# The first stage in feature tiles: rows scaled before they are turned, conditioning columns tile by tile, the first two wide tiles side by side

## The chip, the cores and the metric

The kernel runs on one core of a Trainium2 chip. Inside the core four compute engines work from queues of their own: PE (TensorE, matrix products, with its weight loads shown apart as PEld), DVE (VectorE), ACT (ScalarE) and POOL (GpSimd). SP (SyncE) issues nearly all transfers between HBM and the on-chip memory. The engines meet only at semaphores. The metric is the device time of one launch in microseconds (us); less is better.

## What is computed

One step of a decoder layer for 1024 prompt tokens and 8 sequences of 4 sample tokens, 1056 columns in all, in 32-bit floats. The change touches only what stands before the first wide product and the history that the convolution needs; shortened, the reference reads:

```python
mod = silu(c) @ w_ada + b_ada                    # c: 9 conditioning rows; w_ada: 1024 x 6144
sh1, sc1, g1, sh2, sc2, g2 = split(mod, 6)
h = rmsnorm(x, norm_mix_w) * (1 + sc1) + sh1
z = h @ w_in + b_in                              # 1024 x 8192: q, f, i, og, glu_a, glu_b, gate_a, gate_b
o_a, state = hgrn2_branch(q, f, i, og, lb, hgrn_norm_w, s0)          # 8 heads
o_b, buf = conformer_conv_branch(glu_a, glu_b, buf, dw_w, dw_b, ...) # depthwise, 31 taps, 30 rows of history
x = x + g1 * (concat(sigmoid(gate_a) * o_a, sigmoid(gate_b) * o_b) @ w_out)
h2 = rmsnorm(x, norm_ffn_w) * (1 + sc2) + sh2
gg, uu = split(h2 @ w_ffn_in, 2)
x = x + g2 * ((silu(gg) * uu) @ w_ffn_out)
y = rmsnorm(x, norm_final_w)
```

## The kernel before

Everything is kept feature-major: 128 features on the partitions, 1056 tokens along the free axis, and 8 such feature tiles (`j`) for the 1024 features. Every wide product is made in three passes of rounded operands, high times high, high times low and low times high, so h is needed as `h_hi` and `h_lo`, and each weight block of 1024 x 128 is loaded to `w_raw` (two buffers), rounded on ACT to `w_hi` (`hi`), and its rest is made as `w_lo` (`low`, on DVE in the loop, on POOL for block 0). One wide tile `z_tile` is one block: 8 rows `kt` of 9 products of 352 columns each (3 column groups, 3 passes), in one of the two PSUM tensors `Z`. A head has seven wide tiles, in the order glu_b, glu_a, i, q, f, og, gate_a, and there are 8 heads; tiles and blocks are numbered from 0 through the heads.

**The first stage.** SP loads the conditioning vectors, 9 row tiles `xrow` of x (four buffers), the small vectors, and the first 2048 columns of `w_ada` (`sh1` and `sc1`) in 8 pieces of 256 columns with two buffers `ada_w`. For each row tile PE turns the raw rows (transposes into `Z`, copied by DVE to `xt`), and then multiplies one `ada_w` piece: `ct`, the 9 columns of silu(c), is the stationary operand (a weight load of 9 columns) and 256 columns of `w_ada` stream past it. ACT squares the rows for the mean. Only after all of this come the turning of the conditioning rows, the roots, the row factors made into `ysum`, and then, feature tile by feature tile, h: DVE multiplies (`modulate`), ACT shifts and rounds (`shift_and_round`), POOL makes `h_lo`. The first wide tile waits row by row for `h_ready`; it is followed by the second.

**The order around it.** `load_block(b)` on SP waits for the split of the block whose buffer it takes; for block 1 the code waits for the split of block 0. After the loads SP copies the old history DRAM to DRAM, stores the turned history `ht` to `hist_dram` and x to `xt_dram`, waits for `h_ready` of all tiles, and then enters the loop of the heads (`body`), where behind block 2's place it loads `us`, the history of the head, and `aw`, a piece of `w_ada`. In the loop DVE walks through 28 slots per head, 4 per wide tile. After slot 8 (`CONV_SLOT`) every slot does two of the 31 taps of the convolution (`conv_tap`), until they are done. The recurrence of head h-1 runs in the slots of head h; its parts are small PE jobs between the rows of the wide tiles (`rec_fill`), which DVE and ACT empty. The DVE queue is strictly in the order of the code, so a `low` of the next block stands behind the taps of the tile before.

## Time and profile before

| | |
|---|---|
| Median of three runs | 2049.01 us (2047.14 to 2051.76) |
| Profiled execution, its own time | 2049.11 us |
| Its span in the profile | 2047.4 us |
| PE busy | 1968.2 us, 96% of the span |
| DVE, ACT, POOL busy | 1313.2, 666.9 and 245.4 us |
| Mean granted TensorE clock | 0.985 of full speed |
| First product of wide tile 0 / first product of wide tile 2 | 76.1 us / about 116 us |

The difference between span and time is 1.7 us. The span says how long the engines were at work from the first instruction to the last; the busy share of an engine is its mean over stages that have different limits, so a stage is read by itself: who is idle in it, and what ended each wait. A row of the timeline gives start, duration, engine, line, operation, what was written and read, and in square brackets how long the engine was idle before it and what released it.

### The profile page before, as it was taken

The numbers are of one execution on the slowest core, as the hardware profiler recorded it, in microseconds if no ns is written. First come the engines' busy times: TensorE is split into PE (matmuls) and PEld (weight loads), VectorE is DVE, ScalarE is ACT, GpSimd is POOL, SyncE is SP. The second block draws the span as 40 slices with busy tenths as digits, with TensorE's granted clock in tenths as the row PEclk, the third lists the DMA queues.
The fourth block names the chain that finished last, engine by engine and source line by source line (L and its number), as shares of the span: only waits on it lengthen the run. The fifth ranks groups of instructions, "written<-read, shape, count | busy, mean of one in ns | idle before, by whom it ended". The sixth has DMA issues, their size and how long they took to land.

```text
span 2047.4 us, 39363 instructions
## 1 busy us (share of the span) xinstructions
PE 1968.2 (96%) x15960; PEld 1886.6 (92%) x15960; DVE 1313.2 (64%) x1792; ACT 666.9 (33%) x1070; POOL 245.4 (12%) x245
## 2 busy tenths in 40 slices
PE   7699999999999999999989999999999999999997
PEld 3499999999999999998988989999999999999997
DVE  2776978787887878787575655545445554455444
ACT  2421222323131313132563333333333333333332
POOL 0430010101010001011131654700000000000000
PEclk9799999999999999999989999999999999999998
DMA  8422222223232232223267544444444544445442
GB/s 260 154 75 56 75 76 75 77 70 83 63 87 65 68 84 66 75 73 91 87 199 225 156 121 137 134 136 138 135 135 144 152 131 139 134 141 152 140 135 92
DMA packets 408485, 237.32 MB, mean 116 GB/s; under 512 B 16167, under 2 KB 402887, under 8 KB 408320
## 3 DMA queue, kind: packets, MB, share of 16 engines
q1 hardware_dynamic: 408336, 235.20, 38.9%
...
## 4 chain that ended last, share of the span: by engine, by line
PE 83%; DVE 8%; DMA 3%; ACT 3%; POOL 2%; issue 1%; SPq 0%; DVEq 0%; ACTq 0%; POOLq 0%
PE Z L809 72%; PE R L834 2%; PE R L756 1%; PE R L890 1%; DVE w_lo L1184 1%; DMA ada_w<-in_w_ada_dram 1%; ACT w_hi L1665 1%; PE R L840 1%; DMA w_raw<-in_w_out_dram 1%; DVE ta L1349 1%; PE R L916 1%; PE R L923 1%; DVE k L1213 1%; PE R L925 1%; DVE x L1553 1%
## 5 line engine op out<-in xcount | busy, mean ns | idle before, releaser
L809 PE MATMUL Z<-h_hi,w_hi 128*128 128x352 f32 x2592 | 695.5, 333 | 19.6 <-POOL h_lo L1954 17.0
L809 PE MATMUL Z<-h_hi,w_lo 128*128 128x352 f32 x2592 | 672.0, 323 | 0.0
L809 PE MATMUL Z<-h_lo,w_hi 128*128 128x352 f32 x2592 | 671.1, 323 | 0.0
L1665 ACT ACTIVATE w_hi<-w_raw 128x1024 fp32r<-128x1024 f32 (+1 forms) x316 | 329.4, 1043 | 944.3 <-PE Z L809 923.1
L1184 DVE TENSOR_TENSOR w_lo<-w_raw,w_hi 128x1024 fp32r<-128x1024 f32 (+1 forms) x306 | 376.5, 1230 | 383.8 <-ACT w_hi L1665 375.6
L809 PEld LDWEIGHTS Z<-h_hi,w_hi 128*128 128x128 f32 x2592 | 451.4, 189 | 39.6 <-issue 26.3
L809 PEld LDWEIGHTS Z<-h_hi,w_lo 128*128 128x128 f32 x2592 | 462.9, 189 | 0.0
L809 PEld LDWEIGHTS Z<-h_lo,w_hi 128*128 128x128 f32 x2592 | 461.1, 189 | 0.0
L1332 DVE SCALAR_TENSOR_TENSOR yb<-up,vec,yb 128x1024 f32 (+1 forms) x240 | 308.3, 1285 | 29.8 <-DVE yb L1332 3.7
L809 PE MATMUL Z<-act_hi,w_hi 128*128 128x352 f32 x528 | 170.4, 323 | 0.0
L809 PE MATMUL Z<-act_hi,w_lo 128*128 128x352 f32 x528 | 169.7, 321 | 0.0
L809 PE MATMUL Z<-act_lo,w_hi 128*128 128x352 f32 x528 | 169.5, 321 | 0.0
L809 PEld LDWEIGHTS Z<-act_hi,w_lo 128*128 128x128 f32 x528 | 99.4, 188 | 0.0
L2017 POOL TENSOR_TENSOR gate<-ta,tb 128x1056 f32<-128x1056 f32 x8 | 20.9, 2610 | 654.8 <-ACT ta L1727 654.8
L809 PEld LDWEIGHTS Z<-act_lo,w_hi 128*128 128x128 f32 x528 | 99.3, 188 | 0.0
L809 PEld LDWEIGHTS Z<-act_hi,w_hi 128*128 128x128 f32 x528 | 99.2, 188 | 0.0
L1586 DVE TENSOR_TENSOR tb<-ta,Z 128x352 f32<-128x352 f32 x66 | 34.4, 521 | 74.4 <-PE Z L809 74.2
L809 PE MATMUL Z<-m_hi_b,w_hi 128*128 128x352 f32 x192 | 64.9, 338 | 11.4 <-DVE w_lo L1184 8.8
L809 PE MATMUL Z<-m_hi_a,w_hi 128*128 128x352 f32 x192 | 63.8, 332 | 6.3 <-DVE w_lo L1184 4.0
L809 PE MATMUL Z<-m_hi_b,w_lo 128*128 128x352 f32 x192 | 63.9, 333 | 0.0
L809 PE MATMUL Z<-m_lo_b,w_hi 128*128 128x352 f32 x192 | 63.5, 331 | 0.0
L809 PE MATMUL Z<-m_hi_a,w_lo 128*128 128x352 f32 x192 | 63.2, 329 | 0.0
...
## 6 DMA issues: line engine op xcount, KB each, us to landing
w_raw<-in_w_ffn_in_dram SPq DMA_DIRECT2D x132, 512.0 KB, 3.8
w_raw<-in_w_in_dram SPq DMA_DIRECT2D x64, 512.0 KB, 5.0
w_raw<-in_w_out_dram SPq DMA_DIRECT2D x48, 512.0 KB, 4.0
w_raw<-in_w_ffn_out_dram SPq DMA_DIRECT2D x48, 512.0 KB, 3.8
aw<-in_w_ada_dram SPq DMA_DIRECT2D x32, 512.0 KB, 4.0
...
```

What stands on the lines that cost most here:

```text
L756: last = mm(R[n % 2][0:NSEQ, 0:2 * P], ct[:, kt, 0:NSEQ], ada_w[n % 2][:, kt, :], start=kt == 0, stop=kt == NJ - 1)
L809: last = mm(out, w[:, kt, :], x(kt, g), start=first and kt == 0 and m == 0, stop=last_block and kt == n - 1 and m == 2)
L834: return transpose(out, in_, ident[0:m, 0:m])
L840: last = mm(bank[group:group + 32, ADA_COL:ADA_COL + P], ct[:, kt, :], aw[:, kt, :], start=kt < 4, stop=kt >= 4)
L890: last = mm(bank[p:p + BAND, c * w:(c + 1) * w], k[:, t:t + BAND], halves(qd[:, t:t + BAND], 1 << lv, 1), start=True, stop=True)
L916: last = mm(bank[:, c * P:(c + 1) * P], ktok[:, cc, :], vtok[:, cc, :], start=True, stop=True)
L923: last = mm(out, att[:, cc, :], vtok[:, cc, :], start=True, stop=cc == 0)
L1184: st.tell(V.tensor_tensor(w_lo[b.par][:, 0:n, :], w_raw[b.par][:, 0:n, :], w_hi[b.par][:, 0:n, :].bitcast(F32), ALU.subtract), w_split, b. ...
L1332: ins = V.scalar_tensor_tensor(yp, xp, w, yp, ALU.mult, ALU.add)
L1586: st.tell(V.tensor_tensor(a, sg, Z[t.par][:, 1, 0:GW], ALU.mult), *zfree(t))
L1665: A(w_hi[b.par][:, 0:n, :], w_raw[b.par][:, 0:n, :], ACT.Copy).then_inc(w_hi_ready, 1)
L2017: st.tell(Q.tensor_tensor(gate[:, :], ta[:, :], tb[:, :], ALU.mult), gate_ready, h.v)
```

## The change

- **Rows are scaled token-major.** ACT squares a row tile; POOL makes the reciprocal root of its mean with a power (two instructions of one column per row tile); DVE scales the rows (`xn`, 128 x 1024). PE turns both the raw rows and the scaled rows; ACT copies the raw ones to `xt`, DVE the scaled ones to `xh`. The turning of the factors, the roots on ACT and `ysum` as a row of factors are gone.
- **Conditioning by feature tile.** `ada_w` holds, for one feature tile, 128 columns of `sh1` and 128 of `sc1`, in three buffers. PE multiplies with `w_ada` as the stationary operand (weight loads of 128 columns) and 9 columns of `ct` streaming: 16 products per feature tile. The result stands feature-major at once, so the 16 transposes of the conditioning rows are gone.
- **h by feature tile.** DVE adds the bias (two instructions), makes `am`, and forms h in a buffer from `xh`; ACT makes `h_hi` straight from `xh`; DVE, not POOL, makes `h_lo`. ACT rounds blocks 0 and 1 right after the first `h_hi`; POOL makes `w_lo` of both.
- **The first two wide tiles side by side.** After the conditioning of tiles 0 and 1, each step `kt` is: conditioning of tile `kt + 2`, row `kt` of wide tile 0, row `kt` of wide tile 1.
- **The history is moved.** Its turning stands in slots 8 to 11 of head 0 (the rows of wide tile 2), and in head 0 SP stores it and loads `us` after block 3 is issued, not before block 2. In head 0 DVE's sample part of the convolution stands in slot 14 and the taps begin in slot 12.
- SP issues the stores of x and the copy of the old history behind the last `ada_w` and `hrow` loads.

The diff, cut to its core:

```diff
-CONV_SLOT = 8
+CONV_SLOT, CONV_SLOT0, TAP_SLOT0 = 8, 14, 12
+N_TURNS = 2 * (NC + 1)
+XN = 8
+WADA = 3
+HIST_SLOT = 2 * SLOTS
...
+            def load_mod(j):
+                if j >= WADA:
+                    sp.wait_ge(ada_done, j - WADA + 1)
+                for sec in (SH1, SC1):
+                    sp.dma_start(ada_w[j % WADA][:, sec, :, :], wada_v[:, :, sec * D + j * P:sec * D + (j + 1) * P]) \
+                        .then_inc(adaw_loaded[j % WADA], 16)
...
+            load_mod(0)
+            for t in range(XBUF, NC + 1):
+                load_x(t)
+            load_mod(1)
+            for b in range(2):
+                load_block(Idx(b), win_v[:, :, ORDER[b] * D:ORDER[b] * D + P])
+            for j in range(2, NJ):
+                load_mod(j)
             old = state_conv[0].rearrange("(two s) w d -> two (s w) d", two=2)
             for m in range(2):
                 sp.dma_start(hrow[:, m, :], old[m]).then_inc(hrow_loaded, 16)
...
+            sp.wait_ge(x_evac, N_TURNS)
+            sp.dma_start(xt_dram.rearrange("j p t -> p j t"), xt[:, :, :]).then_inc(xt_stored, 16)
             sp.dma_start(cv_sample[0, :, 0:HIST - LS, :], state_conv[0, :, LS:HIST, :]).then_inc(hist_copied, 16)
...
+            sp.wait_ge(ada_done, NJ)
             sp.wait_ge(h_ready, NJ)
...
-                    if j == 1:
+                    if j == (3 if first else 1):
+                        if first:
+                            sp.wait_ge(hist_evac, 4)
+                            sp.dma_start(hist_dram.rearrange("j p w -> p j w"), ht[:, :, :]).then_inc(ht_stored, 16)
+                            sp.wait_ge(ht_stored, 16)
                         wait(sp, conv_done, h.v)
...
+            def conditioning(j):
+                pe.wait_ge(adaw_loaded[j % WADA], 32 * (j // WADA + 1))
+                if j < 2:
+                    pe.wait_ge(p0_evac, 2)
+                wait(pe, mod_read, j - 1)
+                for sec in (SH1, SC1):
+                    for kt in range(NJ):
+                        last = mm(R[j % 2][:, sec * 16:sec * 16 + NSEQ], ada_w[j % WADA][:, sec, kt, :],
+                                  ct[:, kt, 0:NSEQ], start=kt == 0, stop=kt == NJ - 1)
+                last.then_inc(ada_done, 1)
+            def first_tiles():
+                pe.wait_ge(x_evac, N_TURNS)
+                pe.wait_ge(xn_evac, N_TURNS)
+                for j in range(2):
+                    conditioning(j)
+                for kt in range(NJ):
+                    if kt + 2 < NJ:
+                        conditioning(kt + 2)
+                    if kt == 0:
+                        pe.wait_ge(w_split, 2)
+                    pe.wait_ge(h_ready, kt + 1)
+                    for b in range(2):
+                        for m, (w, x) in enumerate(((w_hi[b], h_hi), (w_hi[b], h_lo), (w_lo[b], h_hi))):
+                            for g in range(G):
+                                last = mm(Z[b][:, g, 0:GW], w[:, kt, :], x[:, kt, g * GW:(g + 1) * GW],
+                                          start=kt == 0 and m == 0, stop=kt == NJ - 1 and m == 2)
...
             for j in range(NJ):
-                shift_and_round(hbuf[j % 3], TP, T, h_hi[:, j, :], SH1 * NJ + j, h_full, j + 1, h_hi_ready)
+                act.wait_ge(am_ready, j + 1)
+                A(h_hi[:, j, 0:TP], xh[:, j, 0:TP], ACT.Identity, bias=mod[:, SH1 * NJ + j, 0:1], scale=am[:, j, 0:1])
+                act.wait_ge(h_full, j + 1)
+                A(h_hi[:, j, TP:T], hbuf[j % 3][:, TP:T], ACT.Copy).then_inc(h_hi_ready, 1)
+                if j == 0:
+                    for b in range(2):
+                        hi(Idx(b))
...
-            low(Idx(0))
-            for j in range(NJ):
-                pool.wait_ge(h_hi_ready, j + 1)
-                st.tell(Q.tensor_tensor(h_lo[:, j, :], hbuf[j % 3][:, 0:T], h_hi[:, j, :].bitcast(F32), ALU.subtract),
-                        h_ready, j + 1)
+            for t in range(NC + 1):
+                m = tokens(t)
+                pool.wait_ge(x_squared, t + 1)
+                st.do(Q.tensor_scalar(ms9[0:m, t:t + 1], ms9[0:m, t:t + 1], 1.0 / D, EPS, ALU.mult, ALU.add))
+                st.settle()
+                st.tell(Q.tensor_tensor(rs9[0:m, t:t + 1], ms9[0:m, t:t + 1], mhalf[0:m, t:t + 1], ALU.pow),
+                        rms_ready, t + 1)
+            for b in range(2):
+                low(Idx(b))
```

**Three places in the order of the instructions.** On PE, the end of the first stage before (the numbers behind names tell buffers apart; `crow` to `ta` and `tb` are the conditioning rows, `rs` the row factors):

```order
L767 MATMUL Z<-ident,xrow_134 128x128 x8
L756 MATMUL R<-ada_w_130,ct 9x256 x8
L767 MATMUL Z<-ident,xrow_131 128x32 x8
L779 MATMUL Z<-ident,hrow 128x120 x16
L785 MATMUL Z<-ident,ta 128x9 x8
L785 MATMUL Z<-ident,tb 128x9 x8
L793 MATMUL Z<-ident,rs_81 128x128 x8
```

On PE after, from the last row tile to the first rows of the two wide tiles:

```order
L765 MATMUL Z<-ident,xn 128x128 x8
L765 MATMUL Z<-ident,xn 128x32 x8
L790 MATMUL R<-ct,ada_w_135 128x9 x16
L790 MATMUL R<-ct,ada_w_136 128x9 x16
L790 MATMUL R<-ct,ada_w_137 128x9 x16
L809 MATMUL Z<-h_hi,w_hi_67 128x352 x3
L809 MATMUL Z<-h_lo,w_hi_67 128x352 x3
L809 MATMUL Z<-h_hi,w_lo_69 128x352 x3
L809 MATMUL Z<-h_hi,w_hi_68 128x352 x3
L809 MATMUL Z<-h_lo,w_hi_68 128x352 x3
L809 MATMUL Z<-h_hi,w_lo_70 128x352 x3
L790 MATMUL R<-ct,ada_w_135 128x9 x16
```

The products with `ada_w` left the row tiles; they stand between the rows of the wide tiles, with `ct` streaming past them. On SP, the last loads of the first stage and what follows them before:

```order
L460 DMA w_raw_63<-in_w_in_dram 128x8x128
L460 DMA w_raw_64<-in_w_in_dram 128x8x128
L509 DMA out_dram<-in_state_conv_dram 8x2x13312
L511 DMA hist_scratch<-ht 128x8x240
L512 DMA xt_scratch<-xt 128x8x1056
L586 DMA us<-hist_scratch 128x8x30
L522 DMA aw<-in_w_ada_dram 128x8x128
L460 DMA w_raw_63<-in_w_in_dram 128x8x128
L460 DMA w_raw_64<-in_w_in_dram 128x8x128
```

On SP after, first the stretch around block 1, which is `w_raw_66`:

```order
L492 DMA ada_w_136<-in_w_ada_dram 128x8x128 x2
L473 DMA w_raw_65<-in_w_in_dram 128x8x128
L473 DMA w_raw_66<-in_w_in_dram 128x8x128
L492 DMA ada_w_137<-in_w_ada_dram 128x8x128 x2
L492 DMA ada_w_135<-in_w_ada_dram 128x8x128 x2
L492 DMA ada_w_136<-in_w_ada_dram 128x8x128 x2
L492 DMA ada_w_137<-in_w_ada_dram 128x8x128 x2
```

and then the stretch from the history rows on:

```order
L520 DMA hrow<-in_state_conv_dram 120x1024 x2
L522 DMA xt_scratch<-xt 128x8x1056
L523 DMA out_dram<-in_state_conv_dram 8x2x13312
L473 DMA w_raw_65<-in_w_in_dram 128x8x128
L473 DMA w_raw_66<-in_w_in_dram 128x8x128
L595 DMA hist_scratch<-ht 128x8x240
L598 DMA us<-hist_scratch 128x8x30
L530 DMA aw<-in_w_ada_dram 128x8x128
L473 DMA w_raw_65<-in_w_in_dram 128x8x128
L473 DMA w_raw_66<-in_w_in_dram 128x8x128
```

Six of the eight `ada_w` pairs stand behind block 1; the store of `ht`, the load of `us` and that of `aw` moved from ahead of block 2 to ahead of block 4. On DVE, head 0 from the read of wide tile 1 on, before:

```order
L1184 TENSOR_TENSOR w_lo_68<-w_raw_64,w_hi_66 128x1024
L1363 SCALAR_TENSOR_TENSOR up<-Z,vec,tb 128x1056
L1366 COPY us<-up 128x8x4
L1349 TENSOR_TENSOR ta<-us,vec 128x992
L1351 TENSOR_REDUCE yb<-ta 128x32
L1354 TENSOR_SCALAR yb<-yb,vec 128x32
L1329 TENSOR_SCALAR yb<-up,vec 128x1024
L1332 SCALAR_TENSOR_TENSOR yb<-up,vec,yb 128x1024 x5
L1184 TENSOR_TENSOR w_lo_67<-w_raw_63,w_hi_65 128x1024
L1332 SCALAR_TENSOR_TENSOR yb<-up,vec,yb 128x1024 x8
L1184 TENSOR_TENSOR w_lo_68<-w_raw_64,w_hi_66 128x1024
```

and after:

```order
L1215 TENSOR_TENSOR w_lo_70<-w_raw_66,w_hi_68 128x1024
L1394 SCALAR_TENSOR_TENSOR up<-Z,vec,tb 128x1056
L1397 COPY us<-up 128x8x4
L1429 COPY ht<-R 128x480 x4
L1215 TENSOR_TENSOR w_lo_69<-w_raw_65,w_hi_67 128x1024
L1360 TENSOR_SCALAR yb<-up,vec 128x1024
L1363 SCALAR_TENSOR_TENSOR yb<-up,vec,yb 128x1024 x3
L1380 TENSOR_TENSOR ta<-us,vec 128x992
L1382 TENSOR_REDUCE yb<-ta 128x32
L1385 TENSOR_SCALAR yb<-yb,vec 128x32
L1363 SCALAR_TENSOR_TENSOR yb<-up,vec,yb 128x1024 x4
L1215 TENSOR_TENSOR w_lo_70<-w_raw_66,w_hi_68 128x1024
```

The four copies of `ht` came in, and the taps (`yb<-up`) stand behind the `low` of block 4, where 6 of them stood ahead of it.

## Rows read from the trace of the kernel before

**Rows 1.** The page's first part: busy time, share of the span, instructions.
```profile
PE 1968.2 (96%) x15960; PEld 1886.6 (92%) x15960; DVE 1313.2 (64%) x1792; ACT 666.9 (33%) x1070; POOL 245.4 (12%) x245
```

**Rows 2.** Stretches: length, busy of each engine, granted clock, DMA share, GB/s.
```profile
60.00:76.00 16.00, 6.04 (x41) 5.43 (x38) 12.47 (x27) 5.06 (x7) 5.16 (x3) 0.59 0.75 265
76.00:98.00 22.00, 13.91 (x54) 12.60 (x54) 19.81 (x23) 12.50 (x18) 13.91 (x6) 0.76 0.28 112
100.00:102.00 2.00, 1.84 (x8) 1.38 (x7) 0.08 (x1) 0.00 (x0) 1.76 (x2) 0.58 0.00 0
```

**Rows 3.** ACT's timeline: ends of wide tiles 1, 2 and 6, block 2.
```profile
110.05 1.06 ACT L1665 ACTIVATE w_hi<-w_raw 128x1024 fp32r<-128x1024 f32 x1 [10.09 <-DMA w_raw<-in_w_in_dram]
...
116.11 1.06 ACT L1665 ACTIVATE w_hi<-w_raw 128x1024 fp32r<-128x1024 f32 x1 [2.55 <-PE Z L809]
127.79 1.06 ACT L1665 ACTIVATE w_hi<-w_raw 128x1024 fp32r<-128x1024 f32 x1 [10.62 <-PE Z L809]
...
174.38 1.06 ACT L1665 ACTIVATE w_hi<-w_raw 128x1024 fp32r<-128x1024 f32 x1 [9.56 <-PE Z L809]
```

**Rows 4.** The chain that ended last, in order of time, to wide tile 2.
```profile
58.22 0.61 PE Z L767 x8
...
101.76 28.34 PE Z L809 x168
```

**Rows 5.** ACT's timeline: one square with its sum; one copy from PSUM.
```profile
4.88 1.06 ACT L1682 ACTIVATE xsq<-xrow 128x1024 f32<-128x1024 f32 x1 [0.72 <-DMA xrow<-in_x_prompt_dram]
5.84 0.19 ACT L1682 ACTIVATION_READ_ACCUMULATOR xsq<-xrow 128x1 f32 x1
...
177.67 0.60 ACT L1743 ACTIVATE vtok<-R 128x512 f32<-128x512 f32 x1 [1.21 <-PE R L834]
```

**Rows 6.** SP's timeline: loads of blocks, stores, loads of `us` and `aw`.
```profile
48.89 14.49 SPq L460 DMA_DIRECT2D w_raw<-in_w_in_dram  x2
...
101.87 0.64 SPq L586 DMA_DIRECT2D us<-hist_scratch  x1
```

**Rows 7.** DMA issues: KB each, median us from issue to landing.
```profile
w_raw<-in_w_ffn_in_dram SPq DMA_DIRECT2D x132, 512.0 KB, 3.8
xt_scratch<-xt SPq DMA_DIRECT2D x1, 4224.0 KB, 20.4
hist_scratch<-ht SPq DMA_DIRECT2D x1, 960.0 KB, 10.5
```

**Rows 8.** PE timeline: weight loads that small products wait for; products at half clock.
```profile
981.06 2.06 PEld L955 LDWEIGHTS R<-ones,ysum 128*128 128x128 f32 x18
...
60.54 0.57 PEld L785 LDWEIGHTS Z<-ident,ta 9*128 9x128 f32 x8 [0.15 <-issue]
...
84.99 1.08 PE L809 MATMUL Z<-h_lo,w_hi 128*128 128x352 f32 x3
85.87 1.08 PE L809 MATMUL Z<-h_hi,w_lo 128*128 128x352 f32 x3
```

**Rows 9.** POOL's and DVE's timeline: POOL splits or multiplies, DVE beside it.
```profile
60.64 2.34 POOL L1939 TENSOR_TENSOR w_lo<-w_raw,w_hi 128x1024 fp32r<-128x1024 f32 x1 [58.76 <-ACT w_hi L1665]
...
176.61 2.47 POOL L2017 TENSOR_TENSOR gate<-ta,tb 128x1056 f32<-128x1056 f32 x1 [53.79 <-ACT ta L1727]
...
177.73 2.46 DVE L1190 TENSOR_TENSOR qd<-q,f 128x1056 f32<-128x1056 f32 x1 [1.03 <-PE R L834]
```

**Rows 10.** DVE's timeline in head 0; PE's first diagonal job of head 1.
```profile
119.98 2.16 DVE L1349 TENSOR_TENSOR ta<-us,vec 128x992 f32<-128x992 f32 x1
...
123.55 0.81 DVE L1329 TENSOR_SCALAR yb<-up,vec 128x1024 f32<-128x1024 f32 x1
...
142.58 1.22 DVE L1184 TENSOR_TENSOR w_lo<-w_raw,w_hi 128x1024 fp32r<-128x1024 f32 x1
...
145.06 10.54 DVE L1332 SCALAR_TENSOR_TENSOR yb<-up,vec,yb 128x1024 f32<-128x1024 f32 x8
...
188.16 0.76 PE L880 MATMUL R<-q,k 128*32 128x32 f32 x64
```

More of the change, by code:

```diff
@@ L351, in program @@
     x_loaded = [sem(f"x_loaded{i}") for i in range(XBUF)]
-    adaw_loaded, adaw_used, adaw_read = two("adaw_loaded"), sem("adaw_used"), sem("adaw_read")
+    adaw_loaded = [sem(f"adaw_loaded{i}") for i in range(WADA)]
+    ada_done, mod_read, am_ready = sem("ada_done"), sem("mod_read"), sem("am_ready")
+    x_turned, x_evac, xn_scaled, xn_turned, xn_evac = (
+        sem("x_turned"), sem("x_evac"), sem("xn_scaled"), sem("xn_turned"), sem("xn_evac"))
+    hist_turned, hist_evac = sem("hist_turned"), sem("hist_evac")
     csig_ready, c_ready, x_squared = (
@@ L742, in _ @@
             last.then_inc(p0_done, 1)
-            pe.wait_ge(rows_loaded, 16 * 12)
-            bank, col = fill0(P0_VEC), 0
-            for tile, n in enumerate((NVA, NVB, NDW // 2, NDW // 2)):
-                last = transpose(bank[:, col:col + n], vrow[0:n, tile, :], ident[0:n, 0:n])
-                col += n
-            last.then_inc(p0_done, 1)
-            def ada_cols(n):
-                pe.wait_ge(adaw_loaded[n % 2], 16 * (n // 2 + 1))
-                if n >= 2:
-                    pe.wait_ge(adaw_read, n - 1)
-                for kt in range(NJ):
-                    last = mm(R[n % 2][0:NSEQ, 0:2 * P], ct[:, kt, 0:NSEQ], ada_w[n % 2][:, kt, :],
-                              start=kt == 0, stop=kt == NJ - 1)
-                last.then_inc(adaw_used, 1)
@@ L760, in _, with vectors, turn @@
-            pe.wait_ge(p0_evac, P0_C + 1)
+            def vectors():
+                pe.wait_ge(rows_loaded, 16 * 12)
+                col = 0
+                for tile, n in enumerate((NVA, NVB, NDW // 2, NDW // 2)):
+                    last = transpose(R[1][:, col:col + n], vrow[0:n, tile, :], ident[0:n, 0:n])
+                    col += n
+                last.then_inc(p0_done, 1)
+            def turn(t, row, normed, done, read):
+                m = tokens(t)
+                for n in range(2 * t, 2 * t + 2):
+                    wait(pe, read, n - 2)
+                    bank = turn_bank(normed, n)
+                    for j in range(4):
+                        last = transpose(bank[:, j * m:(j + 1) * m], row[0:m, (4 * (n % 2) + j) * P:(4 * (n % 2) + j + 1) * P],
+                                         ident[0:m, 0:m])
+                    last.then_inc(done, 1)
@@ L827, in small @@
             def small(fill):
-                if not (fill.i is None and fill.n < 2):
+                if fill.i is None and fill.n < 2:
+                    pe.wait_ge(hist_evac, 4)
+                else:
                     pe.wait_ge(*evac(fill + (-2)))
@@ L965, in slot @@
                     at[0] += 1
-                for j in range(NT):
-                    first = h.i is None and h.n == 0 and j == 0
-                    z_tile(t0 + j, slot, (1, 3, 5, 7), (lambda kt: pe.wait_ge(h_ready, kt + 1)) if first else None)
+                for j in range(2 if first else 0, NT):
+                    z_tile(t0 + j, slot, (1, 3, 5, 7))
             heads(pe, body, lambda: None)
@@ new lines, in normed_evac @@
+            def normed_evac(t):
+                for n in range(2 * t, 2 * t + 2):
+                    dve.wait_ge(xn_turned, n + 1)
+                    st.tell(V.tensor_copy(turned(xh, n), turn_bank(1, n)[:, 0:4 * tokens(t)].rearrange(
+                        "p (j t) -> p j t", j=4)), xn_evac, n + 1)
+            for t in range(NC + 1):
+                m = tokens(t)
+                dve.wait_ge(rms_ready, t + 1)
+                wait(dve, xn_turned, 2 * (t - XN + 1))
+                st.tell(V.tensor_scalar(xn[0:m, t % XN, :], xrow[t % XBUF][0:m, :], rs9[0:m, t:t + 1], None, ALU.mult),
+                        xn_scaled, t + 1)
+                if t:
+                    normed_evac(t - 1)
+                if t == 3:
+                    first_evac(1, vec[:, :], R[1][:, 0:NVEC])
+                    lower_bounds_in()
@@ L1380, in body @@
                 hh = h + (-1)
+                first = h.i is None and h.n == 0
+                conv_at, taps_from = (CONV_SLOT0, TAP_SLOT0) if first else (CONV_SLOT, CONV_SLOT + 1)
                 for j in range(NT):
-                    low(t0 + (j + 1))
+                    if not (first and j == 0):
+                        low(t0 + (j + 1))
                     if j:
@@ L1764, in body @@
                 for j in range(NT):
-                    hi(t0 + (j + 1))
+                    if not (h.i is None and h.n == 0 and j == 0):
+                        hi(t0 + (j + 1))
                     if j:
```

278 lines of the change are left out of this document (113 added, 165 removed).

## The prediction

> **What bounds the kernel now.** I read the page first: PE is busy 96% of the span [rows 1], so a gain needs PE idleness that ends earlier. I looked for it in the stretches, then in the waits and the chain. The first stage is where it lies. Between 60 and 76 us PE is busy 6 of 16 us, and between 76 and 98 us 14 of 22, at 0.59 and 0.76 of its clock [rows 2]: wide tile 0 waits row by row for `h_lo`. The chain shows PE still at the row tiles at 58 us and free of waits only from 101.8 us on [rows 4]. From there the timeline of ACT, which rounds a block as soon as PE has left its buffer, marks the tiles: wide tile 1 ends at 116.1 us, tile 2 at 127.8, so a tile is 11.67 us or 0.162 us a product, and tile 6 ends at 174.4 [rows 3]. PE reaches head 1's diagonal job at 188.2 [rows 10]. These three points, 116.1, 174.4 and 188.2, are what I compare with; behind the last one both kernels run the same code in step.
>
> **Row tiles.** ACT becomes the longest queue: a square with its sum 1.15, two copies from PSUM at 0.60 [rows 5]. Nine squares 10.4, the copies of seven tiles before the last square 8.4, the two exponentials with their table load 1.7 (an estimate from their kind), about 1.0 lost early because PE turns at half clock; from the first square at 4.9 the last one ends at 26.3. Behind it come the power on POOL, the scaling, eight small transposes and two copies: 3.3, so the stage ends at 29.6. The power is not in this stage before; bounds for the end are 27.5 and 33.
>
> **Conditioning.** 16 products of 32-bit operands are 32 passes. Each loads 128 columns and streams 9. Two rows bound a pass: 18 passes with full weight blocks took 2.06 us, 0.11 each, while 8 transposes with 9-row weights took 0.57, 0.062 each [rows 8]. I take 0.11, since its blocks are the same, and 3.6 us per feature tile; the other gives 2.0. Before, this work lay under the loads; now seven of the eight are on the path. The Trainium skill (TensorE: Matmul & The Clock Gate, LDWEIGHTS) has a load cost its columns over 1.2 GHz whatever its rows, 107 ns here; that is against turning the operands round, and by it 32 passes would be 3.4 us. The 9-row trace row disagrees with it, the 128-row one agrees.
>
> **What SP holds back.** Block 1 waits for block 0's split: before, two issues of blocks lasted 14.5 us for that [rows 6]. Now the `ada_w` pairs of tiles 2 to 7 all stand behind it. From `ada_done` of tile 0 at 33.2: about 2.2 for the bias, `am` and h on DVE, 1.05 to round block 0 [rows 3], 2.35 on POOL [rows 9], 3.8 to load block 1 [rows 7], 1.05 and 2.35 again, 0.2 between: 13.0, so 46.2. The third `ada_w` pair lands then too, three 512 KB loads behind each other. PE idles from 36.8 to 46.3.
>
> **The two tiles together.** PE restarts at half clock, where three products take 0.88 us instead of 0.49 [rows 8]; conditioning 2 takes 5.3 then and ends at 51.6. Five times a pair of rows (18 products, 2.92) and a conditioning (3.6) end at 84.2, three pairs more at 93.0. DVE, with about 4 us per feature tile, hides in 6.5, as do loads of 1 MB. The last `h_ready` is at 88.1; block 2 lands 3.8 later, is rounded when tile 0 has left its buffer (93.0), and tile 2 starts near **95.0**, 0.8 of it for semaphores. Before that was 116.1, so 21.1 is gained up to here. The store of x, history rows and the copy go out from 65 us on: 7.0 MB, where 6.0 MB before took 21 us up to the landing of x [rows 7], so they end near 89, just when block 2 is issued; 1 to 3 us more belong to the range.
>
> **What comes back: history.** Tile 2 now has 16 transposes between its rows, 4 jobs of about 0.44: 13.4 us instead of 11.67. DVE has emptied them at +14.2 (counted from tile 2's start). SP waits for that with `us`, `aw` and block 4 queued behind. The store of 960 KB took 10.5 us beside others, and a 512 KB transfer takes 3.8 [rows 7]; alone I take 6.3, ends 3.8 and 10.5. From the issue of `us` to the block behind `aw` being rounded it was 8.2 before, 101.87 [rows 6] to 110.05 [rows 3]. So block 4 is there at +28.8 and split at +31.2. PE would need it at +25.1: 6.1 us of idleness.
>
> **What comes back: taps.** DVE does `low` of block 4 before its taps, so all 31 begin at +31.2. Eight taps are 10.54, `low` and the read of q 2.48, the sample part 3.57 [rows 10]. Tile 3's slots: 4.75 + 3.6 + 5.25 + 2.5 = 16.1; the next two: 10.5 + 1.15 + 1.6 (f and k) + 10.5 + 2.5 = 26.3. PE's tile 7 can start when they are done, at +73.6, where 58.3 stood between the two points before. It is the DVE queue that paces PE there, 13 us a tile against 11.67. Tile 7 starts at 168.6, 5.8 ahead. Then seven taps (9.2), `low` (1.2) and the start of the recurrence (1.7) are 12.1, below PE's 13.8 to the diagonal job. But the gate product, 2.47 on POOL, now falls beside the taps, and a copy of `yb` on POOL beside `low`. When the gate ran beside a DVE product, that took 2.46 [rows 9], against 1.3 for one of its size. Both POOL instructions together are worth between 0 and 4.9; I take 4.6, as the DVE queue has no slack there. Diagonal job at 95.0 + 73.6 + 16.7 = 185.3, **2.9 us ahead** of 188.2.
>
> **The sum.** Span 2047.4 plus 1.7 around it is 2049.1 for the profiled execution, 0.1 from the median. 2049.1 - 2.9 = **2046.2 us**. So 21 us are won in the first stage and 18 are given back in heads 0 and 1.
>
> **Rivals.**
> - *Half clock in the conditioning (slower).* Before, PE fell to 0.58 after gaps between rows [rows 2]. If weight loads with 9 streaming columns do not hold the clock, rows 0 to 7 and conditionings 3 to 7 run partly at half: all of it costs 8 x 2.4 + 5 x 3.5 = 36.5, half of it 18. 2057 to 2083. It decides from 7 us of such work on (2.9 + 4.1). For it: the gaps of [rows 2]. Against: PE has no true gaps here. The Trainium skill names such a thing (the same page, HAM oscillation): waits between bursts of products throttle PE again and again. By it the 3.6 us would count as a wait only if they are no activity, which no row shows.
> - *The history store takes 10.5 as before, and block 2 shares the queue with x's store:* + 4.2 + 2, 2050 to 2055.
> - *Light coupling:* POOL doesn't hold DVE up, -3.1 (PE's 13.8 binds), or a conditioning pass is nearer 0.062: -1.6 six times, 9.6, cut to some 8 by block 2. 2035 to 2043.
> - *The taps don't pace PE,* because DVE catches up during the wait for block 4: only 6.1 + 1.7 of the 21 come back, 2036, with a quicker store 2033. Against: `low` of block 4 is ahead of the taps in the queue.
> - *It doesn't do what it says:* the loads are not spread over the rows at all, since all wait for block 1. That is in the sum already.
>
> **Chances.** Forecast 0.45, own range 2043.5 to 2050; half clock 0.16; slow store 0.16; light coupling 0.17; taps free 0.06. About 0.2%, 4.1 us, is what a measurement of this kernel tells from no change. Faster by more (below 2045.0): 0.13 of the forecast, all light and free, 0.36. Slower by more (above 2053.1): half clock and half of the slow store, 0.24. Within: 0.40. The range 2037 to 2054 leaves out half clock and the ends of the others, 0.2 in all.
>
> **What would show it.** Last square near 26 and the first product of wide tile 0 near 51.6; POOL's second split ending near 46; a conditioning of 3.6 with granted clock 1.00 between 52 and 93; tile 2's first product at 95; block 4 rounded 29 behind it, PE idle about 6 there; taps in 13 us a tile and PE's waits for DVE before tiles 5 and 7; the diagonal job at 185. I am wrong if the clock is half between 52 and 93, if DVE's queue isn't full from block 4 to tile 8, or if the store lands in under 4 us.

## The result and the profile after

The changed kernel takes 2061.85 us, the median of four runs (2060.03 to 2062.85). The kernel before, measured beside it, takes 2049.34 us (2047.14 to 2051.76). The ratio is 1.0060, with a 95% interval of 1.0048 to 1.0073: slower by 12.5 us. The forecast was 2046.2 us and its range ended at 2054, so it was wrong, and the kernel became slower where the forecast had it faster. The profiled execution has a span of 2059.7 us and a mean granted clock of 0.977, where the kernel before has 2047.4 and 0.985.

The page's first line of after answers to [rows 1]. PE is busy 19.5 us longer, with only 166 more instructions.

```profile
PE 1987.7 (97%) x16126; PEld 1926.4 (94%) x16126; DVE 1312.6 (64%) x1806; ACT 666.3 (32%) x1078; POOL 233.6 (11%) x256
```

The stretches of after answer to [rows 2]; the columns are the length, the busy time of each engine with its number of instructions, the granted clock, the DMA share and GB/s.

```profile
34.00:44.00 10.00, 9.74 (x46) 9.64 (x46) 3.24 (x9) 2.35 (x3) 2.48 (x1) 0.50 0.02 5
44.00:50.00 6.00, 0.00 (x0) 0.00 (x0) 1.55 (x7) 2.31 (x3) 1.23 (x1) 0.50 1.01 257
...
60.00:76.00 16.00, 16.00 (x95) 16.00 (x94) 4.43 (x9) 1.81 (x4) 0.00 (x0) 0.71 0.45 126
76.00:98.00 22.00, 22.00 (x134) 22.00 (x135) 9.05 (x21) 4.21 (x6) 0.00 (x0) 0.78 0.93 324
```

PE is busy without a break from 60 to 98 us, which the change was to bring about, but at 0.71 and 0.78 of its clock. Worse, in the ten microseconds from 34 on PE and its weight loads are both busy 96% of the time or more, and the clock is at 0.50, its level of 1.2 GHz. The same stretch of the kernel before, where 256 columns of `w_ada` stream past each load of `ct` and rows are turned in between, reads:

```profile
34.00:44.00 10.00, 9.62 (x53) 4.68 (x51) 4.19 (x8) 1.78 (x4) 0.00 (x0) 1.00 0.90 301
```

There PE is as busy, its weight loads half as much, and the clock is at 1.00. That is the first sign of the cause.

The chain that ended last shows the order of events in after: start, length, then the engine, tile and line. It answers to [rows 4]. `R L790` are the conditioning products, `Z L809` rows of wide tiles 0 and 1, `Z L842` rows of the tiles behind them.

```profile
30.54 6.38 PE R L790 x32
40.10 2.48 POOL w_lo L1986
43.64 7.57 DMA ada_w<-in_w_ada_dram
51.26 7.00 PE R L790 x32
58.25 4.71 PE Z L809 x18
62.96 4.37 PE R L790 x32
67.33 5.24 PE Z L809 x18
...
80.59 3.48 PE R L790 x32
...
113.18 3.14 PE Z L842 x18
```

x32 are the 32 passes of one conditioning, x18 a pair of rows. A conditioning takes 6.4 and 7.0 us where the sum had 3.6 and, once, 5.3; between the rows it takes 3.5 to 4.6. A pair of rows takes up to 5.2 where the sum had 2.9. Tile 2 starts at 113.2 instead of the 95.0 of the forecast, only 3 us ahead of the kernel before.

From tile 2 on, PE's timeline has a short wait at its start, three longer ones in head 0 and one before the diagonal job, which answers to the last of [rows 10]. In brackets stands the idle time before the instruction, and what ended it.

```profile
113.18 0.71 PE L842 MATMUL Z<-h_hi,w_hi 128*128 128x352 f32 x3 [1.10 <-DVE w_lo L1215]
...
141.18 1.22 PE L842 MATMUL Z<-h_hi,w_hi 128*128 128x352 f32 x3 [2.93 <-DVE w_lo L1215]
...
157.05 0.75 PE L842 MATMUL Z<-h_hi,w_hi 128*128 128x352 f32 x3 [1.26 <-DVE q L1401]
...
183.16 0.75 PE L842 MATMUL Z<-h_hi,w_hi 128*128 128x352 f32 x3 [2.44 <-DVE tb L1401]
...
198.71 0.75 PE L912 MATMUL R<-q,k 128*32 128x32 f32 x64 [1.38 <-DVE q0s L1224]
```

These are the starts of tiles 2, 4, 5 and 7 and of the diagonal job. From tile 2 to tile 7 it is 70.0 us, from there to the diagonal job 15.5: 85.5 together, where the kernel before has 72.1, from 116.1 to 188.2 [rows 3, 10]. So the diagonal job is 10.5 us late, 2.9 gained before tile 2 and 13.5 lost behind it. In the profiled executions the lag then grows by 1.8 us to 12.3. The cause of that is open. PE waits 5.8 us in all for `m_lo_a` where the merged columns are multiplied, and 2.2 before, but these waits do not explain it: e6_taps has 5.9 us of them and its lag shrinks behind the diagonal job, from 5.0 to 4.4 us.

### The profile page after: what moved, and what is told of

It reads as the page before. It is cut to its first block, busy times and chain, and to the rows that moved or that the text cites. A ratio compares the mean times of both kernels' runs of the same rounds, so it can differ in the third digit from the quotient of the medians.

```text
span 2059.7 us, 39740 instructions
## 1 busy us (share of the span) xinstructions
PE 1987.7 (97%) x16126; PEld 1926.4 (94%) x16126; DVE 1312.6 (64%) x1806; ACT 666.3 (32%) x1078; POOL 233.6 (11%) x256
## 4 chain that ended last, share of the span: by engine, by line
PE 80%; DVE 9%; ACT 3%; DMA 3%; POOL 2%; issue 1%; SPq 0%; DVEq 0%; ACTq 0%; POOLq 0%
PE Z L842 68%; DVE yb L1363 2%; PE R L790 2%; PE Z L809 2%; DVE w_lo L1215 2%; PE R L866 2%; PE R L922 1%; ACT w_hi L1706 1%; DMA w_raw<-in_w_out_dram 1%; PE R L872 1%; DVE ta L1380 1%; PE R L948 1%; PE R L955 1%; DVE k L1244 1%; PE R L957 1%
## 5 line engine op out<-in xcount | busy, mean ns | idle before, releaser
L842 PE MATMUL Z<-h_hi,w_hi 128*128 128x352 f32 x2544 | 683.7, 332 | 10.2 <-DVE w_lo L1215 4.9
L842 PE MATMUL Z<-h_hi,w_lo 128*128 128x352 f32 x2544 | 660.5, 323 | 0.0
L842 PE MATMUL Z<-h_lo,w_hi 128*128 128x352 f32 x2544 | 659.2, 322 | 0.0
L842 PEld LDWEIGHTS Z<-h_hi,w_hi 128*128 128x128 f32 x2544 | 442.1, 189 | 29.5 <-issue 18.5
L842 PEld LDWEIGHTS Z<-h_hi,w_lo 128*128 128x128 f32 x2544 | 453.6, 188 | 0.0
L842 PEld LDWEIGHTS Z<-h_lo,w_hi 128*128 128x128 f32 x2544 | 451.6, 188 | 0.0
L842 PE MATMUL Z<-act_hi,w_hi 128*128 128x352 f32 x528 | 170.2, 322 | 0.0
L842 PE MATMUL Z<-act_hi,w_lo 128*128 128x352 f32 x528 | 169.5, 321 | 0.0
L842 PE MATMUL Z<-act_lo,w_hi 128*128 128x352 f32 x528 | 169.3, 321 | 0.0
L842 PEld LDWEIGHTS Z<-act_hi,w_lo 128*128 128x128 f32 x528 | 99.4, 188 | 0.0
L842 PEld LDWEIGHTS Z<-act_lo,w_hi 128*128 128x128 f32 x528 | 99.2, 188 | 0.0
L842 PEld LDWEIGHTS Z<-act_hi,w_hi 128*128 128x128 f32 x528 | 99.0, 188 | 0.0
L1627 DVE TENSOR_TENSOR tb<-ta,Z 128x352 f32<-128x352 f32 x66 | 34.4, 521 | 74.4 <-PE Z L842 74.2
L842 PE MATMUL Z<-m_hi_a,w_hi 128*128 128x352 f32 x192 | 64.3, 335 | 9.5 <-DVE m_lo_a L1473 5.8
L842 PE MATMUL Z<-m_hi_b,w_hi 128*128 128x352 f32 x192 | 65.0, 339 | 8.0 <-DVE w_lo L1215 8.0
L842 PE MATMUL Z<-m_lo_b,w_hi 128*128 128x352 f32 x192 | 63.7, 332 | 0.0
L842 PE MATMUL Z<-m_hi_b,w_lo 128*128 128x352 f32 x192 | 63.7, 332 | 0.0
L842 PE MATMUL Z<-m_lo_a,w_hi 128*128 128x352 f32 x192 | 63.2, 329 | 0.0
```

Source lines behind the costliest of these rows:

```text
L842: last = mm(out, w[:, kt, :], x(kt, g), start=first and kt == 0 and m == 0, stop=last_block and kt == n - 1 and m == 2)
L1627: st.tell(V.tensor_tensor(a, sg, Z[t.par][:, 1, 0:GW], ALU.mult), *zfree(t))
```

## The experiments

Two questions. Why is the clock low in the first stage: because of what the conditioning passes are, a full weight load with few streaming columns behind it (theory A), or because PE waits between its bursts (theory B)? And what sets the pace behind tile 2: DVE's queue with its taps (theory T), or SP's chain of history store and loads (rival S)? All kernels start from the changed kernel. A pass is one weight load with the columns that stream past it; the 16 products of a conditioning are 32 passes. The table has the median, the ratio to the kernel before with its 95% interval, and from the profiled execution the starts of tile 2 and of head 1's diagonal job.

| kernel | us | ratio to before | tile 2 | diagonal job |
|---|---|---|---|---|
| before | 2049.34 | 1 | 116.1 | 188.2 |
| after | 2061.85 | 1.0060 (1.0048 to 1.0073) | 113.2 | 198.7 |
| e1_cols32 | 2052.41 | 1.0022 (1.0010 to 1.0034) | 106.1 | 192.3 |
| e9_cols64 | 2048.18 | 1.0006 (0.9997 to 1.0016) | 101.1 | 186.6 |
| e2_cols128 | 2043.78 | 0.9980 (0.9968 to 0.9992) | 97.1 | 182.8 |
| e3_fewpass | 2039.24 | 0.9951 (0.9938 to 0.9964) | 88.4 | 176.2 |
| e4_nohold | 2052.12 | 1.0015 (1.0001 to 1.0028) | 104.7 | 190.2 |
| e5_cols_nohold | 2033.20 | 0.9932 (0.9914 to 0.9950) | 87.5 | 173.4 |
| e6_taps | 2052.73 | 1.0013 (1.0001 to 1.0025) | 114.4 | 193.2 |
| e7_hist | 2048.34 | 1.0003 (0.9993 to 1.0014) | 108.9 | 183.1 |
| e8_all | 2023.20 | 0.9874 (0.9857 to 0.9890) | 86.7 | 161.7 |
| e10_no_taps | 2021.24 | 0.9874 (0.9857 to 0.9890) | 85.9 | 160.2 |

Where an effect is given in us below, it is the difference of two ratios times 2049. One caution on single profiles: the first stage of after, e6_taps and e7_hist is the same code, and tile 2 starts at 113.2, 114.4 and 108.9. Where the clock falls and rises differs from one execution to the next by some 5 us, so effects are taken from medians and intervals, and places within one stretch from the profiles.

### How many columns a pass streams

A conditioning pass loads 128 weight columns and streams the 9 columns of `ct`. `ct` is 32 columns wide, the rest zeros, so a pass can stream more without touching the result. e2_cols128 streams it four times over:

```diff
-last = mm(R[j % 2][:, sec * 16:sec * 16 + NSEQ], ada_w[j % WADA][:, sec, kt, :],
-          ct[:, kt, 0:NSEQ], start=kt == 0, stop=kt == NJ - 1)
+last = mm(R[j % 2][:, sec * P:sec * P + P], ada_w[j % WADA][:, sec, kt, :],
+          ct[:, kt, :].unsqueeze(1).to_broadcast([P, 4, 32]), start=kt == 0, stop=kt == NJ - 1)
...
-return V.tensor_scalar(mod[:, sec * NJ + j, :], R[j % 2][:, sec * 16:sec * 16 + NSEQ],
+return V.tensor_scalar(mod[:, sec * NJ + j, :], R[j % 2][:, sec * P:sec * P + NSEQ],
```

> Same kernel as after, but each conditioning pass streams 128 columns (ct's 32, four times over) instead of 9; same weight loads, same order. Theory A (few streaming columns do not hold the clock): granted clock 1.00 from 30 to 44 us; a pass costs between 0.11 (load beside streaming) and 0.17 at full clock, so conditionings 0 and 1 take 3.5 to 5.5 us each instead of 6.6, rows in pairs 2.9 to 3.2; tile 2 starts between 96 and 106 instead of 113.2, time 2045 to 2055. Theory B (the gap for block 1 and the waits between bursts take the clock): 0.50 between 32 and 62 as before, and the passes get longer, 0.25 to 0.3 each, so the time goes up, 2062 to 2085.

e1_cols32 streams the 32 columns once, e9_cols64 twice.

> Same kernel as after, but each conditioning pass streams 32 columns of ct (9 real, 23 zeros) instead of 9; same weight loads, same order. Theory A (few streaming columns do not hold the clock): with three and a half times the columns the granted clock between 32 and 62 us is above 0.50, somewhere up to 1.00; a pass goes from 0.205 to between 0.11 and 0.2, tile 2 starts up to 15 us before 113.2, the time is between 2047 and 2062. If 32 columns are still too few, nothing moves: 2061 to 2063. Theory B (the gap at 44 to 51 us and the waits between bursts take the clock): nothing moves, 0.50 in 32 to 62, 2061 to 2063.

> As e2_cols128, with 64 streaming columns a pass (ct's 32 twice over) instead of 128; everything else as after. It puts a third point between 32 columns, where the clock was at 0.50 from 34 to 60 us, and 128, where it was at 0.92 or more until PE ran dry. If the clock goes by how much of a pass is streaming, 64 columns may hold it: conditionings 0 and 1 in 7.4 us, tile 2 at 96 to 98, time 2042 to 2046. If 64 are too few, the pair takes 9 to 12 us, the first product of wide tile 0 comes at 56 to 58, tile 2 at 99 to 107, time 2046 to 2053.

Measured: 14 times the columns, and the kernel is 16 us faster than after. At 2043.8 us it is even 1 us below the range that theory A had. The chain of e2_cols128, over the same events as above:

```profile
30.71 3.82 PE R L790 x32
37.71 2.48 POOL w_lo L1986
41.23 7.39 DMA ada_w<-in_w_ada_dram
48.66 5.69 PE R L790 x32
54.35 2.88 PE Z L809 x18
57.24 3.57 PE R L790 x32
60.81 2.92 PE Z L809 x18
```

In 34 to 44 us the clock is at 0.92 where after had 0.50, and from 60 to 98 us at 1.00 where after had 0.71 and 0.78:

```profile
34.00:44.00 10.00, 4.09 (x37) 3.90 (x35) 6.16 (x13) 2.35 (x3) 2.46 (x1) 0.92 0.22 56
...
60.00:76.00 16.00, 16.00 (x123) 16.00 (x122) 7.84 (x21) 4.21 (x6) 0.00 (x0) 1.00 0.71 199
76.00:98.00 22.00, 20.36 (x147) 20.09 (x146) 8.84 (x18) 7.32 (x9) 6.72 (x21) 1.00 0.75 280
```

PE is busy no longer than in after in these stretches, and gets more done. The chain now has the very numbers of the forecast, 3.6 for a conditioning and 2.92 for a pair of rows. One conditioning is longer, the 5.69 at 48.66 us: PE has idled from 38.1 us on before it, and in 44 to 50 us the clock is at 0.50. So a wait costs the clock as well; the padding does not change that.

The first group of weight loads, those of conditionings 0 and 1, shows the steps between. In order, after with 9 columns, e1_cols32, e9_cols64 and e2_cols128, from the PEld timeline:

```profile
30.51 13.13 PEld L790 LDWEIGHTS R<-ct,ada_w 128*128 128x128 f32 x64 [0.69 <-issue]
```
```profile
31.36 12.06 PEld L790 LDWEIGHTS R<-ct,ada_w 128*128 128x128 f32 x64 [0.69 <-issue]
```
```profile
30.45 12.10 PEld L790 LDWEIGHTS R<-ct,ada_w 128*128 128x128 f32 x64 [0.69 <-issue]
```
```profile
30.68 7.22 PEld L790 LDWEIGHTS R<-ct,ada_w 128*128 128x128 f32 x64 [0.69 <-issue]
```

With 32 and 64 columns the clock still falls to 0.50 here, and the 64 loads take 12.1 us; the rise that both expectations thought possible for this stretch did not come. The runs differ further on, where rows of the wide tiles stand between the conditionings. In 60 to 76 us, with 32 and then 64 columns:

```profile
60.00:76.00 16.00, 16.00 (x123) 16.00 (x122) 7.29 (x15) 2.93 (x5) 0.00 (x0) 0.98 0.61 171
```
```profile
60.00:76.00 16.00, 16.00 (x127) 16.00 (x126) 6.58 (x15) 2.81 (x4) 0.00 (x0) 1.00 0.63 171
```

The clock is 0.98 and 1.00, where the three kernels with the first stage of after (after, e6_taps, e7_hist) have 0.71 to 0.82. In 76 to 98 it is 0.77 with 32 columns and 1.00 with 64, against 0.66 to 0.81. Of the four kernels only e2_cols128 kept the clock through conditionings 0 and 1, which stand alone. Theory A holds. It is shown that streaming more columns per load keeps the clock in this kernel; what exactly the chip counts was not tested.

The Trainium skill has a remedy for a clock that falls again and again, on its page TensorE: Matmul & The Clock Gate, section HAM oscillation: do all the products of a tile before PE waits again, or pad the short side. It gives it for a kernel whose PE waits for transfers. Padding helped here too, 128 columns for 9, but whether waits are the cause here is the next question.

### The gap before conditioning 2

PE idles 7.6 us before conditioning 2, since SP stands at block 1's load and the `ada_w` pairs behind it are late. Block 1's buffer is free, so its load need not wait:

```diff
-wait_apart(sp, met, w_split, b.v if b.i is None and b.n < 2 else (b + (-1)).v)
+wait_apart(sp, met, w_split, 0 if b.i is None and b.n < 2 else (b + (-1)).v)
```

> Same kernel as after, but block 1 of w_in is loaded without waiting for block 0's split (its buffer is free), so that the ada_w pairs behind it are not held either. Theory A: PE's gap of 7.6 us before conditioning 2 goes to under 3, the passes stay at 0.205 each and the granted clock at 0.50 up to 55 us; first product of wide tile 0 at 51 to 53 instead of 58.1, tile 2 at 106 to 109, time 2055 to 2059. Theory B (the gap took the clock): clock back to 1.00 once it is gone, tile 2 at 95 to 100, time 2044 to 2050.

The gap is gone: the chain of e4_nohold has conditionings 0 to 2 in one piece, 96 passes in 19.3 us, that is 0.20 a pass as before.

```profile
30.90 19.29 PE R L790 x96
50.18 4.26 PE Z L809 x18
```
```profile
34.00:44.00 10.00, 10.00 (x48) 10.00 (x49) 3.60 (x10) 3.30 (x4) 4.28 (x2) 0.50 0.38 107
...
50.00:60.00 10.00, 10.00 (x65) 10.00 (x66) 4.76 (x13) 2.73 (x4) 0.00 (x0) 0.86 0.46 125
60.00:76.00 16.00, 16.00 (x94) 16.00 (x92) 5.63 (x12) 2.18 (x4) 0.00 (x0) 0.70 0.80 219
76.00:98.00 22.00, 22.00 (x117) 22.00 (x117) 7.74 (x19) 5.00 (x8) 1.70 (x7) 0.67 0.52 211
```

PE is busy every moment from 34 to 98 us, and the clock is at 0.50 through the conditionings, rises to 0.86 with the first rows of the wide tiles, and is then at 0.70 and 0.67, as low as in after. Theory B falls: the clock is low without any wait. The Trainium skill's rule on waits between bursts, in the section named above, does not explain this; the rows show half clock where PE never waited. The gap has a price of its own, 9 us, more than the 3 to 7 that I had expected (tile 2 starts at 104.7 where I had 106 to 109), and it is a second cost beside the clock. e5_cols_nohold has both edits.

> Both edits of the head in one: every conditioning pass streams 128 columns, and block 1's load is not held. Theory A (clock and hold are two separate costs of the head, and everything behind tile 2 only shifts): conditionings 0 to 2 follow each other at 3.7 each, first product of wide tile 0 at 43 to 46 instead of 54.1 with the columns alone, two tiles end near 86, tile 2 starts at 87 to 90; the tail keeps its 70.1 to tile 7 and 15.5 to the diagonal job, so that job is at 173 to 176 and the time 2034 to 2037. Theory B (the gain is eaten: the earlier block 2 collides with the store of x and the history rows): tile 2 at 92 to 97, 2038 to 2044.

Tile 2 starts at 87.5, and the time is 26 us below after, 1 us better than the range of theory A here. Apart the two edits gave 16 and 9. So they add up, and neither hides the other.

### Without most of the passes

e3_fewpass leaves out 12 of the 16 conditioning products of each feature tile; the modulation is then incomplete.

```diff
-for kt in range(NJ):
+for kt in (0, NJ - 1):
```

> Leaves out 12 of the 16 conditioning products of every feature tile (only the first and the last block of each sum are multiplied), so the modulation is incomplete; everything else as after. It measures what the passes cost on the path. Theory A: without them the rows of the two wide tiles run at 0.9 to 1.0 after a start at half clock, conditionings cost under 1.7 us, tile 2 starts between 80 and 92 (DVE's 4 us a feature tile or block 2's load are then late), time 2038 to 2050. Theory B: the clock still falls to 0.50 between rows because PE waits for h, tile 2 starts at 90 to 100, time 2048 to 2055.

The time is 22 us below after, in the range that theory A had. The chance to save more is cut by another thing: tiles 0 and 1 end near 77.8, but PE stands until 88.4 for block 2, whose load was issued at 72.6 us behind the store of x and took 13.4 us. From PE's timeline and from the chain:

```profile
88.42 1.22 PE L842 MATMUL Z<-h_hi,w_hi 128*128 128x352 f32 x3 [10.59 <-DVE w_lo L1215]
```
```profile
72.55 13.39 DMA w_raw<-in_w_in_dram
```

The store of x is the likely reason; that was not tested apart. Issued at 61.7 us it took 18.1, so it was under way until 79.8. In the fastest kernel, e10_no_taps, the store was issued at 58.6 us and took 19.5, so it had landed a microsecond before the same load was issued, and the load took 4.3 us:

```profile
79.04 4.34 DMA w_raw<-in_w_in_dram
```

There PE waits 1.6 us before tile 2 all the same, as e8_all and e2_cols128 do, because SP issues block 2 only when the last h is ready. That wait of SP was not tested. e3_fewpass shows two things of the clock besides. PE idles from 33.2 to 45.9 us, and the rows of the first pair run at half clock: the clock is low after a wait too. And from 60 to 76 us it is at 1.00, though the passes stream 9 columns; there are 8 of them between two pairs of rows, where after has 32 and 0.71.

### What paces PE behind tile 2

In all six kernels that leave the taps, the history and the number of passes alone (after, e1_cols32, e2_cols128, e4_nohold, e5_cols_nohold, e9_cols64) the way from tile 2 to the diagonal job takes 85.5 to 86.2 us, wherever tile 2 starts and at whatever clock the first stage ran. Two edits break it up. e6_taps moves 14 of the 31 taps of head 0 into tile 2, where DVE waits for block 4 anyway, and leaves none in tile 6:

```diff
-CONV_SLOT, CONV_SLOT0, TAP_SLOT0 = 8, 14, 12
+CONV_SLOT, CONV_SLOT0, TAP_SLOT0 = 8, 14, 8
+FIRST_TAPS = {8: 2, 9: 2, 10: 2, 11: 8, 12: 1, 13: 1, 14: 1, 15: 1, 16: 2, 17: 1, 18: 2, 19: 1, 20: 2, 21: 1, 22: 2, 23: 2}
...
-                            for tap in (next(taps, None), next(taps, None)):
+                            for tap in [next(taps, None) for _ in range(FIRST_TAPS.get(slot, 0) if first else 2)]:
```

> After, with only the places of head 0's 31 taps changed: 14 of them stand in tile 2 (2, 2, 2 and 8 behind the four history copies, where DVE waits for block 4), the other 17 are spread over tiles 3 to 5, none in tile 6. Theory T (DVE's queue of taps paces PE from tile 4 to head 1's diagonal job): tile 4 still at +28.0 from tile 2, since block 4 waits for the history store, but then three tiles of 11.7, tile 7 at +63 instead of +70.0, and 13.8 instead of 15.5 to the diagonal job, because no tap is left beside the gate product; time 2052 to 2055. Rival S (SP's chain of history store, us, aw and blocks paces PE): tile 7 stays at +68 to +70, 2060 to 2062.

e7_hist has SP load block 4 before it waits for the turned history and stores it:

```diff
-if j == (3 if first else 1):
+if j == (4 if first else 1):
```

> After, with only the history store (and us and aw behind it) moved behind block 4's load in SP's order. Theory T: tile 4 starts at +25.1 from tile 2 instead of +28.0; and since DVE's low of block 4, which stands ahead of the taps, comes 12 us earlier, all taps do too, and tile 7 starts at +60 to +62 instead of +70.0; the seven taps beside the gate product stay, 15.2 to 15.5 to the diagonal job; time 2051 to 2054. Rival S' (only the wait of 3 us at tile 4 goes, the tap queue keeps its pace of 13 a tile from there): tile 7 at +67, 2058 to 2060.

Both confirm theory T. In e6_taps tile 4 still waits 3.2 us, but there is no wait for DVE before tiles 5 and 7 any more; tile 6 ends 65.0 us behind tile 2's start (I had 63 for the start of tile 7), and the diagonal job comes 13.7 behind that, as in the kernel before. SP's order is untouched there, so rival S falls. In e7_hist tile 6 ends at +60.1, where after has +67.6 and its tile 7 waits 2.4 more. From there it is 14.1 us to the diagonal job, not the 15.2 to 15.5 that I had expected: DVE ends the seven taps and the `low` behind them earlier, and PE waits only 0.25 us for it. ACT's timeline shows it, as in [rows 3]: the rounding of a block starts when PE has left the tile before. The last row is the end of tile 6.

```profile
122.09 1.06 ACT L1706 ACTIVATE w_hi<-w_raw 128x1024 fp32r<-128x1024 f32 x1 [12.59 <-PE Z L842]
134.50 1.06 ACT L1706 ACTIVATE w_hi<-w_raw 128x1024 fp32r<-128x1024 f32 x1 [10.32 <-DMA w_raw<-in_w_in_dram]
...
169.05 1.06 ACT L1706 ACTIVATE w_hi<-w_raw 128x1024 fp32r<-128x1024 f32 x1 [9.56 <-PE Z L842]
```

A wait of 3 us was removed and some 11 are gained between tile 2 and the diagonal job (74.2 instead of 85.5). The reason is the order on DVE: `low` of block 4 stands ahead of all taps. In e7_hist it runs at 123.2, 14.3 behind tile 2's start, and in after at +26.6, so the taps run 11 to 12 us earlier. This is theory T against the rival S', which expected 3 us. The kernel is 12 us faster than after; its 2048.3 us lie 3 below the range that theory T had.

The two edits are two ways to the same gain. e8_all has them both with the edits of the head, e10_no_taps leaves the taps where after has them.

> All four edits: 128 columns a pass, block 1's load not held, taps spread as in e6_taps, history store behind block 4 as in e7_hist. If the costs add up (theory A with T): tile 2 at 87 to 90, tile 7 at +60 to +61, diagonal job at +13.8, so 161 to 165 where the kernel before has 188.2; time 2022 to 2028, 1.1 to 1.3% below the kernel before. If one hides another, as when block 2's load beside the store of x becomes the bound, or the history store lands later than us is wanted: 2029 to 2036.

> e8_all without its taps edit: 128 columns, block 1's load not held, history store behind block 4, the 31 taps where after has them. Theory T says that the two tail edits are two ways to the same 10 us (DVE's queue starts its taps early enough in either), so the one alone is enough: tile 2 at 86 to 88, diagonal job 74.2 behind it as in e7_hist, 160 to 163, time 2021 to 2025, the same as e8_all. Rival: the seven taps that stay in tile 6 beside the gate product, and low of block 8 behind them, cost PE what they cost DVE, 2 to 3 us: diagonal job at 164 to 166, time 2025 to 2028.

The two cannot be told apart: both have the ratio 0.9874. In e10_no_taps DVE is the later of the two engines at the diagonal job, but by 0.4 us only, and the clock is full from 34 us on:

```profile
85.87 0.72 PE L842 MATMUL Z<-h_hi,w_hi 128*128 128x352 f32 x3 [1.64 <-DVE w_lo L1215]
...
160.19 0.75 PE L912 MATMUL R<-q,k 128*32 128x32 f32 x64 [0.41 <-DVE q0s L1224]
```
```profile
34.00:44.00 10.00, 9.11 (x79) 8.91 (x79) 8.16 (x13) 4.77 (x6) 4.79 (x2) 1.00 0.83 223
...
60.00:76.00 16.00, 16.00 (x128) 16.00 (x127) 6.45 (x17) 2.81 (x4) 0.00 (x0) 1.00 1.05 374
```

e10_no_taps is the kernel to keep. It differs from after in three places, and is 1.3% (26 us) faster than the kernel before and 38 us faster than after. The three edits apart gave 16, 9 and 12 us, 37 together.

## The prediction, step by step

**Row tiles: right, 0.9 us short.** The last square ends at 27.2 (26.3 predicted), and the first conditioning starts at 30.5 (29.6).

**Conditioning: wrong, and this is the step that failed.** "I take 0.11" a pass holds at full clock: 32 took 3.57 to 3.82 us in e2_cols128. The failure is the assumption that the clock would be full, in the conditionings and in the rows between them. In after a conditioning that stands alone took 6.4 to 7.0 us at a clock of 0.50 to 0.55, not 3.6, and no wait was needed for that (e4_nohold). It is the sign of being wrong that I had named: in the stretches between 52 and 93 us the clock was at 0.50, 0.71 and 0.78. I listed half clock as a rival with 0.16, and wrote against it that "PE has no true gaps here". That argument was wrong in kind: e4_nohold has no gap at all and half the clock, so the absence of gaps speaks neither for nor against it. What the profile of before could have told is that the passes change their shape. Multiplying with `w_ada` went at 1.00 in 34 to 44 us with 256 streaming columns a load. The row that I priced the new form by had one column a load, but only 18 passes of it, 2.06 us at full clock between rows of a wide tile [rows 8]. It gave the price of a pass and said nothing of 64 in a row. A form unseen at that length deserved a chance nearer to one half.

Tile 2 is 18.2 us behind the forecast, 113.2 against 95.0, and the rival's "half of it" was 18. That the two agree is luck. Rows 0 to 7 and conditionings 3 to 7, which the rival counted, lost 11.0 (from 58.2 to 110.6 us, 52.4 where the sum had 41.4). The other 7.2 came where it counted nothing: conditioning 2 started 5.0 late, took 1.7 more, and 0.5 is left.

**What SP holds back: right in kind, slightly short.** POOL's second split ended at 51.1 instead of 46.2, and the third `ada_w` pair landed then. Of the 5 us, 2.8 are the clock again, in conditioning 0, and 0.9 its late start. In e2_cols128, where the clock holds, the split ended at 48.5. I had the hold in the sum, as 9.5 us in which PE idles, but took it as given; without it the kernel is 9 us faster.

**The two tiles together: right where the clock is full.** e2_cols128 has 2.88 to 2.92 a pair and 3.57 a conditioning, and tile 2 at 97.1 against my 95.0.

**History: right mechanism, store over-priced.** Alone the store landed in 4.3 us, not 6.3. Block 4 was rounded at +25.5 (28.8 predicted), split at +27.9 (31.2), and PE idled 2.9 (6.1).

```profile
127.35 4.31 DMA hist_scratch<-ht
133.07 5.58 DMA w_raw<-in_w_in_dram
```

**Taps: right.** From the split of block 4 to tile 7 it is 42.1 us against my 42.4. Behind it 15.5 were needed, and I had 16.7. The seven taps, `low` and the gate on POOL read, on DVE's and then POOL's timeline:

```profile
183.14 11.52 DVE L1363 SCALAR_TENSOR_TENSOR yb<-up,vec,yb 128x1024 f32<-128x1024 f32 x7
194.80 2.07 DVE L1215 TENSOR_TENSOR w_lo<-w_raw,w_hi 128x1024 fp32r<-128x1024 f32 x1
```
```profile
183.18 2.47 POOL L2064 TENSOR_TENSOR gate<-ta,tb 128x1056 f32<-128x1056 f32 x1 [59.78 <-DVE tb L1401]
194.72 1.07 POOL L2071 COPY ysum<-yb 128x1056 f32<-128x1056 f32 x1 [9.07 <-DVE yb L1363]
```

Seven taps alone take 9.2 (eight are 10.53), so the gate costs DVE 2.3, and the copy costs `low` 0.85: 3.2 of the 4.6 that I took. On its page SBUF — State Buffer, section Who interferes with whom, the Trainium skill describes the port pair that DVE and GpSimd share as an exclusive lock, held for a whole instruction. The trace agrees: DVE's group grew by 2.3 us beside a POOL instruction of 2.47.

**The sum.** Tile 2 came 18.2 us later than forecast, the way to the diagonal job was 4.8 shorter (85.5 against 90.3), so that job stood 13.4 behind the forecast, at 198.7 against 185.3. The lag of 10.5 to the kernel before became 12.3 at the end, where I had taken both kernels to run in step; the cause of that is open. Of the two statements of the summary, "21 us are won in the first stage" was wrong, since 3 were, and "18 are given back" was too much, with 13.5. With more columns a pass, and so with the clock that the forecast assumed, e2_cols128 gave 2043.8, inside my own range for the forecast.

**Chances.** The forecast, the slow store and the light coupling all took the clock for granted. What I called likely rested on one unseen thing, and the range ended at 2054 where that rival began at 2057. That 2057 does not follow from its sum either: 18 us on top of the forecast are 2064, and 2057 would be 11. A range of 2037 to 2070 would have been the honest one.
